# Decays moved into a projection, a rotation moved to GpSimd, and a differential inverse moved ahead of the scaling, in a two-block transformer kernel on one core

## The reference, cut to what matters

```python
dt = softplus(dt_raw + dt_bias)                     # per token, 2 directions x 8 heads
a_cs = cumsum(dt * -exp(a_log)); a_last = a_cs[-1]  # in chunks of 128 tokens: the decays
states = einsum(b, exp(a_last - a_cs), dt * x)      # state of each chunk
y = scan(states, exp(a_last), ...)                  # forward and backward
q = q * cos + rot(q) * sin                          # rotary turning; the same for k
s = where(abs(k_pos - q_pos) <= 128, q @ k.T / 8, -inf)   # window attention with a sink
# second block, differential attention: two softmaxes per head
a = p0 - lam * p1
o = a @ v
```

## Time and profile before

| what | value |
|---|---|
| time, median of 3 runs | 3959.19 us (3953.01 to 3960.21) |
| profiled execution: its own time | 3961.22 us |
| its span | 3959.3 us |
| PE busy | 3732.6 us (94%), 18308 matmul instructions |
| DVE busy | 1872.7 us (47%) |
| ACT busy | 829.0 us (21%) |
| POOL busy | 1013.0 us (26%) |
| mean granted PE clock | 0.983 of full speed |

### The profile page before, as it was taken

How to read it: one execution, slowest core, us unless ns; L and a number is a source line. 1 busy time by engine, 2 the same in 40 slices (tenths; PEclk the granted TensorE clock), 3 DMA queues, 4 the chain that set the end, 5 groups by cost and what they waited for, 6 DMA issues and landing times. The chain is left out here.

```text
span 3959.3 us, 47929 instructions
## 1 busy us (share of the span) xinstructions
PE 3732.6 (94%) x18308; PEld 2556.1 (65%) x18308; DVE 1872.7 (47%) x3522; ACT 829.0 (21%) x1685; POOL 1013.0 (26%) x876
## 2 busy tenths in 40 slices
PE   8988779999999999999999999999999999999998
PEld 6876545555475577555554555555887767778887
DVE  3366232222322276887545566645125655143445
ACT  3124111111201265111212000002114611230001
POOL 1301200000023211223332223222142034443443
PEclk9989889999999999999999999999999999999999
DMA  5410499999611100222220332221110022212221
GB/s 213 185 70 12 158 356 394 395 392 391 243 59 44 47 2 11 80 86 97 80 100 23 121 123 107 107 85 54 48 67 31 12 66 85 84 64 96 85 85 54
DMA packets 72446, 476.18 MB, mean 120 GB/s; under 512 B 8288, under 2 KB 9696, under 8 KB 18976
## 3 DMA queue, kind: packets, MB, share of 16 engines
q1 hardware_dynamic: 69008, 462.40, 31.2%
q0 software_dynamic: 2640, 8.65, 0.8%
q10 hardware_dynamic: 576, 2.10, 0.1%
HBM read 468.92 MB, written 4.19 MB: 119 GB/s over the span
## 5 line engine op out<-in xcount | busy, mean ns | idle before, releaser
L1030 PE MATMUL ps<-projected,weight_ring 128*128 128x384 f32 (+1 forms) x672 | 245.8, 521 | 0.0
L3575 PE MATMUL ps<-projected,weight_ring 128*128 128x384 f32 (+1 forms) x768 | 223.0, 434 | 1.2 <-DVE mlp_u L3774 0.7
L2472 DVE SCALAR_TENSOR_TENSOR sb_x_all<-ps,sb_modulation_ada,sb_x_all 128x512 f32<-128x512 f32 x144 | 106.5, 750 | 245.9 <-PE ps L2297 216.3
L1030 PEld LDWEIGHTS ps<-projected,weight_ring 128*128 128x128 f32 x672 | 127.7, 190 | 106.1 <-issue 45.9
L3575 PEld LDWEIGHTS ps<-projected,weight_ring 128*128 128x128 f32 x768 | 144.8, 190 | 62.5 <-issue 3.0
L3575 PE MATMUL ps<-projected,mlp_weight_sums 128*128 128x384 f32 x480 | 166.1, 489 | 0.0
L3575 PE MATMUL ps<-h2b,weight_ring 128*128 128x384 f32 (+1 forms) x512 | 153.4, 444 | 6.5 <-ACT h2b L943 6.5
L2995 DVE SCALAR_TENSOR_TENSOR projected<-projected,sb_vectors 128x497 f32<-128x497 f32 (+26 forms) x270 | 157.8, 649 | 1.6
L2132 POOL DMA_INDIRECT h<-tokens,own_tokens x31 | 31.1, 1003 | 488.0 <-PE ps L2268 429.4
L2855 PE MATMUL ps<-projected,gate_sums 128*128 128x384 f32 (+1 forms) x512 | 150.2, 437 | 5.0 <-POOL gate_sums L3135 5.0
L1446 DVE TENSOR_REDUCE attention_shift<-ps 128x1 f32<-128x768 f32 (+1 forms) x160 | 130.6, 844 | 47.8 <-PE ps L1316 47.8
(11 more groups left out here) (671 smaller groups left out, 7680.1 us busy)
## 6 DMA issues: line engine op xcount, KB each, us to landing
weight_ring<-w_stream SPq DMA_DIRECT2D x217, 1024.0 KB, 5.0
expert_weights<-w_moe SPq DMA_DIRECT2D x125, 1024.0 KB, 23.0
weight_ring<-w_moe SPq DMA_DIRECT2D x40, 1024.0 KB, 23.7
h2b<-w_moe SPq DMA_DIRECT2D x33, 1024.0 KB, 23.1
weight_ring<-w_stream SPq DMA_DIRECT2D x16, 512.0 KB, 3.8
weight_ring<-w_stream SPq DMA_DIRECT2D x16, 384.0 KB, 3.3
sb_x_all<-xT SPq DMA_DIRECT2D x4, 768.0 KB, 6.9
tokens<-h_tokens ACTq DMA_DIRECT2D x4, 512.0 KB, 9.9
```

The costliest lines, as they stand in the source:

```text
L1030: ins = nc.tensor.matmul(core.ps[:, 2 * slot + half, 0:n], w_of(k), h_of(k)[:, a:a + n], start=(first and k == 0), stop=(last and k == chu ...
L2472: v.scalar_tensor_tensor(core.x[:, k, NCTX:T], ps[:, bank, :], core.mods["ada"][:, 40 + k, 1:2], core.x[:, k, NCTX:T], ALU.mult, ALU.add). ...
L3575: ins = nc.tensor.matmul(acc, wq[:, k, :], bq[:, k, :], start=(first and k == 0), stop=(last and k == 3), skip_group_check=True)
```

## The change

It has four parts.

1. The phase `ssd_decay` is gone. Its instructions are a class `Decay` that `seven_phase` calls in `project1`: `arguments` in front of the column sums, `steps` behind them, and the rest inside the first unit. The function tables of ScalarE are loaded once at the start (`preload_act_table_set(LOGS)`). The sums use PSUM bank 6.
2. The phase `rope1` is gone. The tables are loaded at the start of `project1`. In `ssd_tokens` PE rotates one chunk behind each tile's transposes, ScalarE copies it to SBUF, and GpSimd multiplies by the cosine; the transposes have three pairs of banks in turn instead of four. GpSimd multiplies by the sine and adds in `ssd_states` (four chunks) and in `ssd_scan` (two chunks), by `add_turned`.
3. The window mask is no longer loaded (1 MB). VectorE makes two tiles of 128x128 from constants at the start of `window`.
4. In `attention_phase` the reciprocal and the ratio of a differential pair come in front of `scale`, and only the mix stays behind it.

```diff
-def ssd_decay_phase(core, st):
+class Decay:
...
+    def arguments(self, dve):
+        self.link(v.tensor_tensor(st.dt[:, :, :], st.dt[:, :, :], bias, ALU.add))
+        self.link(v.tensor_scalar(pos[:, :, :], st.dt[:, :, :], 0.0, None, ALU.max))
+        v.scalar_tensor_tensor(self.e[:, :, :], pos[:, :, :], -2.0, st.dt[:, :, :], ALU.mult,
+                               ALU.add).then_inc(self.y_ready, 1)
...
+    def functions(self, act):
+        s.preload_act_table_set(LOGS)
+        s.activation(self.rate[:, :], self.core.r("a_log"), ACT.Exp).then_inc(self.e_ready, 1)
+        act.wait_ge(self.y_ready, 1)
+        s.activation(self.e[:, :, :], self.e[:, :, :], ACT.Exp).then_inc(self.e_ready, 1)
+        act.wait_ge(self.u_ready, 1)
+        s.activation(self.lg[:, :, :], self.u[:, :, :], ACT.Ln).then_inc(self.lg_ready, 1)
...
+    def sums(self, pe):
+        pe.wait_ge(self.da_ready, 1)
...
# seven_phase: TensorE, ScalarE, VectorE
+                if dc and i == 0:
+                    dc.sums(pe)
                 sums(i, 3)
                 pe.wait_ge(t_ready, 2)
...
+            if dc:
+                dc.functions(act)
             for i in range(U):
...
+            if dc:
+                dc.arguments(dve)
             column_quarters(nc.vector, b, lo, n, th, t_ready, False)
+            if dc:
+                dc.steps(dve)
...
# ssd_tokens_phase
-                if t >= 4:
-                    pe.wait_ge(x_out, t - 3)
+                if t >= 3:
+                    pe.wait_ge(x_out, t - 2)
...
+                if t >= 2:
+                    pe.wait_ge(rot_out, t - 1)
+                nc.tensor.matmul(ps[:, 6 + t % 2, :], core.c("rot1"), chunks[t][:, NCTX:T], start=True,
+                                 stop=True).then_inc(rot_done, 1)
...
+                pool.wait_ge(rot_done, t + 1)
+                nc.gpsimd.tensor_tensor(chunks[t][:, NCTX:T], chunks[t][:, NCTX:T], tab[:, 0, :], ALU.mult)
...
+def add_turned(core, pool, sin_done, which, chunks, turned_chunks, tab):
+    p = core.nc.gpsimd
+    for n, i in enumerate(which):
+        t, c = turned_chunks[:, i, :], chunks[i][:, NCTX:T]
+        p.tensor_tensor(t, t, tab[:, 1, :], ALU.mult).then_inc(sin_done, 1)
+        pool.wait_ge(sin_done, n + 1)
+        p.tensor_tensor(c, c, t, ALU.add)
...
# attention_phase, VectorE
+                ahead = 0 <= p - 1 < N and pairs[p - 1]["diff"]
+                if ahead:
+                    inverse(p - 1)
                 if p >= 3:
                     scale(p - 3)
-                if 0 <= p - 1 < N:
+                if ahead:
+                    mix(p - 1)
+                elif 0 <= p - 1 < N:
                     inverse(p - 1)
```

More of the change, by code:

```diff
@@ L1459, in inverse, with mix @@
                                             ALU.mult, ALU.mult).then_inc(ratio_ready, 1)
+            def mix(p):
+                keys, b, r = pairs[p]["keys"], 2 * (p % 2), p % 2
+                if pairs[p]["diff"]:
                     dve.wait_ge(ratio_ready, mixes[p])
@@ L1475, in scale @@
                 nc.vector.tensor_tensor(pairs[p]["out"], acc(p), factor(p), ALU.mult).then_inc(o_out, 1)
+            if banded:
+                for side, allowed in enumerate(("prefix", "suffix")):
+                    nc.vector.tensor_scalar(hidden[:, side, :], core.c(allowed), -1.0, BIG, ALU.add, ALU.mult) \
+                        .then_inc(hidden_ready, 1)
+                dve.wait_ge(hidden_ready, 2)
             for p in range(N + 3):
@@ L1765, in _ @@
             core.stream.load(sp)
+        @block.gpsimd
+        def _(pool):
+            add_turned(core, pool, sin_done, range(4, 6), chunks, turned_chunks, tab)
         @block.tensor
@@ L3275, in seven_phase @@
 def seven_phase(core, name, b, lo, n, units, th=None, conv=None, mods=(), burst=0, heads=None, tail=None,
-                sw=None, made=0, ahead=None):
+                sw=None, made=0, ahead=None, decay=None):
     nc, ps, stream = core.nc, core.ps, core.stream
@@ L3433, in _ @@
                 nc.scalar.activation(quarter(i, 1, 1), z, ACT.Copy, scale=f).then_inc(m5_out, 1)
+                if dc and i == 0:
+                    dc.exponentials(act)
                 act.wait_ge(products, 7 * i + 4)
@@ L3464, in _ @@
                 plus(quarter(i, 0, 1), y, quarter(i, 1, 0), f).then_inc(u2_out, 1)
+                if dc and i == 0:
+                    dc.segments(dve)
                 if kq and len(kq.turns.get(i, ())) == 2:
@@ L3470, in _ @@
                 plus(quarter(i, 1, 1), y, quarter(i, 1, 1), f).then_inc(c22_out, 1)
+                if dc and i == 0:
+                    dc.weights(dve)
                 if kq and len(kq.turns.get(i, ())) == 1:
@@ L3879, in first_block @@
             st.z = zq[:, 0:4, :]
+            st.da = sb("dt_rate", [P, TILES, 16], mix)
+            st.acs = sb("running_sum", [P, TILES, 16], mix)
+            st.wdt = sb("state_factor", [P, TILES, 16], mix)
+            st.keep = sb("tile_decay", [P, TILES, 16], mix)
+            tab = cat[:, 6:8, :]
             with ExitStack() as pre:
@@ L3911, in first_block @@
                     st.xw = sb("state_x", [P, 2, TILES, SSD_W], tok)
[L3912 to L3921 removed]
+                    ssd_tokens_phase(core, st, *turning)
+                    ssd_states_phase(core, st, *turning)
+                ssd_scan_phase(core, st, *turning)
+            partly = [(1, 1, 1), (0, 0, 2), (1, 0, 2), (2, 0, 1)]
             pairs = []
@@ L3928, in first_block @@
                                  for r in (0, HD)],
-                        "diff": False, "keys": NCTX + (hi - lo) * P, "tile": t,
+                        "diff": False, "keys": NCTX + (hi - lo) * P,
                         "spans": [(0, NCTX), (NCTX + lo * P, (hi - lo) * P)],
-                        "masked": (CT + partly[t][0] - lo, *partly[t]), "sink": ROW["sinks"][0] + 2 * c,
+                        "masked": (CT + partly[t][0] - lo, *partly[t][1:]), "sink": ROW["sinks"][0] + 2 * c,
                         "v": lambda i, kv=c // 2, lo=lo: v[:, i if i < CT else i + lo, kv * HD:(kv + 1) * HD],
                         "out": cat[:, 4 + c, t * P:(t + 1) * P]})
-            attention_phase(core, "window", pairs, masked=mask, y=cat)
+            attention_phase(core, "window", pairs, banded=True, y=cat)
             dump("cat", cat)
@@ L4290, in rope_tables @@
     return np.stack(out, axis=1).astype(np.float32)
-def window_mask():
-    q = np.arange(NX).reshape(XT, P)
-    k = np.arange(NX)
-    ok = np.abs(k[None, None, :] - q[:, :, None]) <= P
-    return np.where(ok, 0.0, -BIG).astype(np.float32).transpose(1, 0, 2).copy()
 def dft_tables():
```

223 lines of the change are left out of this document (88 added, 135 removed).

## The result

The changed kernel takes 3932.64 us in the median (3930.91 to 3938.35, 5 runs) beside 3960.21 (3953.01 to 3964.35, 5 runs) for the kernel before: a ratio of 0.9929, 95% interval 0.9919 to 0.994. That is 27.6 us less in the medians and 27.4 in the spans of the two profiled executions; 28.8 was forecast, and 3930.4 as the time. The sum came out within 1.4 us, but four of its terms are off by 1.6 to 2.0 us, two in each direction, so that the closeness of the sum is luck in part.

What follows compares the result with a forecast made beforehand. TensorE, busy 94% of the span, was taken as the bound, through its idle and low-clock stretches. Gains of 34.4 us less 5.6 given back made 28.8 net, so 3930.4 us, range 3923 to 3941.

Steps and rivals of the forecast that it cites:

- Decay stage, 8.6: Between project1 and the token stage: removing the decay stage gains 8.6 us.
- First unit, 3.6: In project1's first unit: the added decays cost 3.6 us, a 2.4 us TensorE stall plus 1.2 for three matmuls.
- Rival 2: Decays dearer: small instructions each held behind a GpSimd add, 8.5 us in place of 3.6; 3937.1 us, chance 0.14.
- Rope stage, 11.8: Ahead of the window attention: removing the rope stage gains 11.8 us.
- scan, 0.7 back: In ssd_scan: four added GpSimd instructions hold a VectorE instruction that TensorE's first products wait for, costing 0.7 us.
- Window, 2.0: At the window's start: TensorE comes busy instead of at the low clock, gaining 2.0 us (between 0 and 3).
- States, 1.3 back: In ssd_states: eight added GpSimd instructions slow VectorE's chain, partly offset by an earlier start; cost 1.3 us (0 to 3).
- Attention, 12.0: In both attentions: the mix starts sooner after the scaling, cutting TensorE's waits; gain 12.0 us (0 to 14.0).
- Rival 1: The attention gains nothing because another wait takes the mix's place; 3942.4 us, chance 0.10.
- rival 4: Slower than before: the attention's reciprocal waits for late exponentials and holds scaling, mix and TensorE; 3967 us, chance 0.02.
- rival 5: TensorE waits as long behind the token stage as in the decay stage, costing at most 8.6; 3939 us, chance 0.04.
- Rival 3: TensorE keeps its clock in the states and the window's thin steps, 4 us more gained; 3926.4 us, chance 0.08.

Runs made afterwards that it cites:

- order alone: The kernel before with only the attention's reciprocal and ratio put ahead of the scaling; ratio 0.9968, 12.7 us less.
- second and third trace of the changed kernel: The changed kernel run again unaltered, two more times; ratios 0.9932 and 0.9929 against the kernel before.
- the later sums' second: Second run of the changed kernel with the three matmuls of the sums two products later in project1's first unit; ratio 0.9911.
- filled wait: The changed kernel with ten matmuls nobody reads in front of TensorE's wait for dt_rate in project1's first unit; one execution took 3939.22 us.

## Why the prediction was right, term by term

- **Decay stage, 8.6:** 8.55 (8.88 became 0.33).
- **First unit, 3.6:** project1 grew by 5.58. The stall was 2.98 (2.4 forecast; 3.14 by the starts of the groups): three of the seven instructions were held by GpSimd, not one. The sums took 0.75 (1.2). The step that failed is "at full speed I take 1.2": I let the clock stand through a stall. The two groups behind it lost 1.7, and 3.14 + 0.75 + 1.7 is the 5.58. With the rope stage back, where the clock stood through the same stall, the growth is 3.97, near the forecast. The price varies: against "order alone", which like them has no low stretch in unit four, the second and third trace of the changed kernel grew by 6.9 and 7.2. Rival 2 had the direction, with a cause (GpSimd's additions) that makes 0.6 of it, not 4.9.
- **Rope stage, 11.8; scan, 0.7 back:** the scan with what follows fell by 9.31, so 2.5 came back: 0.86 up to the last head, and 1.66 by the clock's fall, for which the forecast had nothing.
- **Window, 2.0:** 3.6. The start gives 1.9 (4.39 us to the first transposes, 6.27 before). The rest is a second stretch at the low clock, from about 338.4 in the kernel before, that none of the three traces of the changed kernel has: there eight scores took 2.08 us where such take 1.14 now. The forecast did not have this part; it is luck.
- **Tokens, 0:** 0.2 gained. **States, 1.3 back:** 0.5 gained in the first trace and 1.3 back in the two others. Both halves of that step, GpSimd's price and the clock's gift, are confirmed by the table; the price is paid each time, and whether the gift comes varies from execution to execution.
- **Attention, 12.0:** 11.1 by the stages. Period 3.76, not 3.84. By the starts of VectorE's mix, before and with the order alone, 22 steps with 768 keys gain 0.37 each, 8.3 in all, where 31 at 0.31 were forecast; the others stand next to pairs without a mix and gain little or nothing. The pairs with 256 keys gain 2.3 (2.4 forecast). A step was worth more than forecast, and fewer steps gained.
- **The mask**, nothing: it was not tried alone; the kernel with the rope stage back shows no gain by it.

From project1 to window the first trace is 16.6 us shorter where the terms give 16.8. All other stages together, which the change does not touch, differ by 0.2, out of parts of up to 3.1. Rival 1 is out (the order alone), rival 4 too (VectorE's waits for exponentials ahead of the reciprocal stay below 0.4 us in each attention), rival 5 too (0.53 us). Rival 3, the kept clock, came true in the window each time and in the states once in three.

What remains open is what decides whether the clock falls behind an idle stretch of 2 to 3 us. The same 1.94 us in front of the last head were followed by a fall in five traces and by none in two others with the same code there (the later sums' second, and the filled wait's). The 3.0 us in the first unit had a fall behind them in four traces of five, and the 2.06 us ahead of the out projection in six of thirteen.

## What to carry to other kernels

A chain of small instructions taken into a busy stage is free only if its consumer on the bound engine stands late enough: look for the place in that engine's queue at which the result is already there, and put it behind, not at the first place where it may stand. A stall of TensorE of 3 us cost its length and, in four traces of five, 1.7 to 3.2 us more by the clock, so a term that leaves or removes one needs both, the second as a chance. With falls moving between stages, compare stage by stage with several traces, and count as gained what repeats. No run here shows a gain of time from filling a wait with useless matmuls.

## What the runs showed of the hardware

- Behind a stall of 3 us 1.89 us of matmuls became 3.54 to 3.67 in four traces, with the granted clock at its lower level, and 1.92 in a fifth, where it stayed up. With the stall filled by work that nobody reads it was 1.92 too, in one trace.
- The same idle stretch has or has not a fall behind it: 2.06 us ahead of the out projection (2.82 us for the next eight matmuls in seven traces, 4.20 to 5.46 in six), 2.90 in unit four of `project1`, where the eight behind it take 2.62 us in one trace of the changed kernel and 1.99 in another, by the rows of the timeline.
- VectorE's `TENSOR_SCALAR` with one SBUF input was held by GpSimd too: 1.29 us beside L3143, 0.21 alone.
- Which of the two is held depends on who comes first, and some 0.1 us decides it: a wait of TensorE behind VectorE's taps was 2.9 us long in eleven traces and 1.9 in two.
